# Rotary tiles rotated one by one through three places, evictions in another order, six mixing banks, and the softmax weights of both heads on VectorE

## The reference

```python
proj = rmsnorm_2(x, norm_g) @ w_in
(a_q, a_k, a_v, a_g, b_q, b_k, b_v, b_g, i_q, i_k, i_w, c_q, c_k, c_v, c_g, m_g) = split(proj)
ya = moba_attention(rope(a_q), rope(a_k), a_v) * silu(a_g)             # 6 heads: causal softmax here
yb = dsa_attention(rope(b_q), rope1(b_k), b_v, rope(i_q), rope1(i_k), i_w) * silu(b_g)   # 6 heads, 256 keys picked
# 12 heads in 3 groups of dilation 1, 4, 16; each gives an output o_g and a log-sum-exp lse_g:
yc = sum_g softmax_over_g(lse_g) * o_g                                 # "the mixing"
yc = yc * silu(c_g)
merged = sigmoid(m_g0)*(ya @ w_br_a) + sigmoid(m_g1)*(yb @ w_br_b) + sigmoid(m_g2)*(yc @ w_br_c)
x = x + merged @ w_out
# apply_rope: concat([x1*c - x2*s, x1*s + x2*c]) on the halves x1, x2 of each head's 64 channels
```

## Time and profile before

| | |
|---|---|
| median of 3 runs | 3239.16 us (3238.86 to 3243.96) |
| profiled execution, its own time | 3240.51 us |
| its span in the profile | 3238.8 us |
| TensorE (PE) busy | 3096.6 us (96%) |
| VectorE (DVE) busy | 1712.2 us (53%) |
| ScalarE (ACT) busy | 1190.6 us (37%) |
| GpSimd (POOL) busy | 251.5 us (8%) |
| mean granted TensorE clock | 0.98 |

### The profile page before, as it was taken

One profiled execution on the slowest core, in us unless ns is written; L12 is line 12 of the kernel. 1 busy time (PEld: TensorE's weight loads), 2 busy tenths in 40 slices (PEclk: granted clock), 3 DMA queues, 4 the chain that ended last, 5 costly groups with the idle time before them and its releaser, 6 DMA issues.

```text
span 3238.8 us, 38745 instructions
## 1 busy us (share of the span) xinstructions
PE 3096.6 (96%) x16353; PEld 2597.7 (80%) x16353; DVE 1712.2 (53%) x2370; ACT 1190.6 (37%) x1574; POOL 251.5 (8%) x324
## 2 busy tenths in 40 slices
PE   6999999999999999999999999899899999898999
PEld 5888888888888988888798888777777897676788
DVE  6555553345555653347753334688654357865434
ACT  3222255642122422236732223334562233455422
POOL 0000011210000000001200000122210001311000
PEclk8999999999999999999999999899999999999999
DMA  6555522114555352323222322332222224322222
GB/s 229 182 177 187 169 79 65 53 53 169 199 183 170 119 187 91 104 78 108 78 92 91 101 94 68 96 90 74 85 72 78 91 66 123 85 79 66 78 92 72
DMA packets 287270, 354.23 MB, mean 109 GB/s; under 512 B 9546, under 2 KB 263290, under 8 KB 287098
## 3 DMA queue, kind: packets, MB, share of 16 engines
q1 hardware_dynamic: 287098, 351.75, 33.6%
HBM read 336.52 MB, written 2.10 MB: 105 GB/s over the span
## 4 chain that ended last, share of the span: by engine, by line
PE 80%; DVE 11%; ACT 5%; POOL 1%; issue 1%; DMA 1%; SPq 0%; DVEq 0%; ACTq 0%; POOLq 0%
PE psum L655 50%; PE psum L814 6%; PE psum L1202 5%; PE psum L772 3%; PE psum L1294 3%; PE psum L676 2%; PE psum L696 1%; DVE w_low L1909 1%; ACT area L1709 1%; PE psum L912 1%; DVE area L2369 1%; PE psum L1176 1%; DVE area L2415 1%; DVE psum L2058 1%; DVE mod_acc L2425 1%
## 5 line engine op out<-in xcount | busy, mean ns | idle before, releaser
L655 PE MATMUL psum<-h_high,w_high 128*128 128x512 f32 (+1 forms) x1936 | 757.1, 391 | 8.0 <-DVE w_low L1909 5.0
L655 PE MATMUL psum<-h_high,w_low 128*128 128x512 f32 (+1 forms) x1936 | 753.4, 389 | 0.0
L655 PE MATMUL psum<-h_low,w_high 128*128 128x512 f32 (+1 forms) x1936 | 753.4, 389 | 0.0
L1909 DVE TENSOR_TENSOR w_low<-raw,w_high 128x2048 fp32r<-128x2048 f32 (+3 forms) x246 | 547.1, 2235 | 315.3 <-ACT w_high L1352 315.3
L1352 ACT CAST w_high<-raw 128x2048 fp32r<-128x2048 f32 (+4 forms) x254 | 464.8, 1843 | 570.2 <-DMA raw<-in_ffn_w_gu 237.4
L655 PEld LDWEIGHTS psum<-h_high,w_high 128*128 128x128 f32 (+1 forms) x1936 | 362.6, 187 | 88.9 <-issue 8.7
L655 PEld LDWEIGHTS psum<-h_high,w_low 128*128 128x128 f32 (+1 forms) x1936 | 362.6, 187 | 77.0
L655 PEld LDWEIGHTS psum<-h_low,w_high 128*128 128x128 f32 (+1 forms) x1936 | 362.7, 187 | 76.4 <-issue 1.0
L655 PE MATMUL psum<-y_high,w_high 128*128 128x512 f32 x592 | 233.0, 394 | 7.3 <-DVE y_low L2095 3.4
L2181 DVE TENSOR_TENSOR area<-area,psum 128x512 f32<-128x512 f32 x88 | 60.2, 684 | 336.9 <-PE psum L655 328.5
L655 PE MATMUL psum<-y_high,w_low 128*128 128x512 f32 x592 | 231.4, 391 | 0.0
(11 more groups left out here) (312 smaller groups left out, 5185.4 us busy)
## 6 DMA issues: line engine op xcount, KB each, us to landing
raw<-in_ffn_w_gu SPq DMA_DIRECT2D x88, 1024.0 KB, 6.1
raw<-in_mod_w SPq DMA_DIRECT2D x64, 1024.0 KB, 5.0
raw<-in_w_in SPq DMA_DIRECT2D x64, 1024.0 KB, 5.2
raw<-in_ffn_w_down SPq DMA_DIRECT2D x32, 1024.0 KB, 7.5
raw<-in_ffn_w_down SPq DMA_DIRECT2D x16, 768.0 KB, 4.8
raw<-in_sb_w_qkv SPq DMA_DIRECT2D x12, 1024.0 KB, 5.2
area<-area SPq DMA_DIRECT2D x92, 128.0 KB, 2.3
raw<-in_lru_w_in SPq DMA_DIRECT2D x10, 1024.0 KB, 5.4
```

The costliest lines, as they stand in the source:

```text
L655: mm = e.matmul(psum[0:width, base + m, :], wv[a][:, at_k, c0:c0 + width], X[b][:, k, :], start=(at_k == 0 and (a, b) == (0, 0)), stop=(at ...
L1909: e.tensor_tensor(w_low[raw_at[m]][:, :n], raw[raw_at[m]][:, :n], w_high[x % NW][:, :n].bitcast(F32), ALU.subtract).then_inc(*q.up(s_low, ...
```

## The change

1. **Three places by tiles.** The tiles to be rotated or turned in the heads go round through three places (`L.x_at`): the two of `rope_x` and one more. A tile waits only for the tile three before it (`x_tile_free`, `tile_left`). The swap is of one tile, four DMAs of half the size, with a semaphore for each half of `rope_y`; it waits for the eviction and for the previous rotated unit's same half (`y_tile_free`).
2. **VectorE's rotations** (`rope_tile`) of all that was made beside p-1 stand together in round p, behind `row_max` and ahead of `lows` and `weights`. GpSimd's `rope_begin` waits for the eviction and no longer for the swap.
3. **Evictions.** ScalarE evicts turned values at the head of the round where they lead the list; only one product, and only in rounds with more than two items beside, is evicted between the two `exps`; the other products of the first list are evicted behind `turned_copy(p)`.
4. **Weights.** VectorE scales both heads' weights; GpSimd's `weights` is gone.
5. **Mixing.** The three pairs of banks are taken at once and all six matmuls are issued in a row.

```diff
@@ -565,10 +572,37 @@
...
+            places = [L.rope_x[:, 0, :], L.rope_x[:, 1, :], spare(0, 5, 6)[:, 0, :]]
+            in_heads = [(name, c0, m) for name, c0 in order[order.index(("a_v", 256)) + 1:] for m in range(2)]
+            L.x_at = {tile: places[i % 3] for i, tile in enumerate(in_heads)}
+            def tile_left(name, c0, m):
+                if name == "c_v" or (name, c0, m) == ("b_q", 256, 1):
+                    turned = [("tile_turned", stage, name, c0, m)]
+                    if name == "c_v":
+                        return turned
+                else:
+                    turned = []
+                return turned + [("swapped", stage, name, c0, m), ("rope_cos", stage, name, c0, m)]
+            def x_tile_free(name, c0, m):
+                at_ = in_heads.index((name, c0, m))
+                if at_ >= 3:
+                    return tile_left(*in_heads[at_ - 3])
+                return x_left("a_v", 256) + x_left("a_k", 128)
+            def y_tile_free(name, c0, m):
+                before = rotated[rotated.index((name, c0)) - 1]
+                return [("roped", stage, *before, m)]
+            L.x_tile_free, L.y_tile_free = x_tile_free, y_tile_free
...
-                return [x_left(*order[-1]), y_left(*rotated[-1]), [("past", (stage, "heads"), x) for x in ENGINES]][b]
+                return [[step for tile in in_heads[-3:] for step in tile_left(*tile)], [("roped", stage, *rotated[-1], m) for m in range(2)], [("past", (stage, "heads"), x) for x in ENGINES]][b]
@@ -1260,16 +1292,17 @@
...
+                pairs = [take_pair() for _ in range(3)]
+                q.wait_ge(*at("mix_weights", stage))
+                q.wait_ge(*at("mix_sel", stage))
...
-                    b = base_of["mix", stage, m] = take_pair()
-                    q.wait_ge(*at("mix_weights", stage))
-                    q.wait_ge(*at("mix_sel", stage))
...
-                        if g == 2:
-                            q.wait_ge(*at("mixed", stage, m, 0))
-                        e.matmul(psum[:, b + g % 2, :], L.sel[0:4, m, :], L.lse_rows[g], start=True, stop=True).then_inc(
+                        bank = base_of["mix", stage, m, g] = pairs[m] + g if g < 2 else pairs[2] + m
+                        e.matmul(psum[:, bank, :], L.sel[0:4, m, :], L.lse_rows[g], start=True, stop=True).then_inc(
...
-                    free_pair(b, ("mixed", stage, m, 2))
+                    free_pair(pairs[m], ("mixed", stage, m, 2))
+                free_pair(pairs[2], ("mixed", stage, 1, 2))
@@ -1736,14 +1769,12 @@
...
-                        for before in L.x_free(name, c0):
+                        for before in L.x_tile_free(name, c0, m):
...
-                        dst, dil = L.rope_x[:, m, :], L.dilation(name, c0) if what == "rope" else (1, 4, 16)[c0 // PANEL]
+                        dst, dil = L.x_at[name, c0, m], L.dilation(name, c0) if what == "rope" else (1, 4, 16)[c0 // PANEL]
...
-                        if what == "rope" and last:
-                            q.mark("roped_in", stage, name, c0)
@@ -1789,25 +1820,36 @@
...
-                    first = L.beside[p][0]
+                    first, second = L.beside[p]
+                    turned = [item for item in first if item[0] == "turn"]
+                    made = [item for item in first if item[0] == "product"]
+                    needed = made[:1] if made[:1] == first[:1] and len(first) + len(second) > 2 else []
...
+                    if first[:1] == turned[:1]:
+                        for item in turned:
+                            evict(*item)
...
-                    for item in first[:1]:
+                    for item in needed:
...
-                    for item in first[1:]:
-                        evict(*item)
+                    if first[:1] != turned[:1]:
+                        for item in turned:
+                            evict(*item)
...
+                    for item in made:
+                        if item not in needed:
+                            evict(*item)
@@ -2392,6 +2434,25 @@
...
+                def rope_tile(name, c0, m):
+                    dil, rows = L.dilation(name, c0), L.parts(name, c0)[m]
+                    src, cos, sin = L.x_at[name, c0, m][0:rows, :], rope_c[0:rows, :], L.rope_y[0:rows, m, :]
+                    to = L.dests[name, c0][m][0:rows, :]
+                    if dil > 1:
+                        src, cos, sin = (a.rearrange("p (j r) -> p j r", r=dil) for a in (src, cos, sin))
+                        to = to.rearrange("p (r j) -> p j r", r=dil)
+                    if m:
+                        q.wait_ge(*at("evicted", stage, "product", name, c0, m))
+                        if (name, c0) in L.place_of:
+                            for x in range(2):
+                                q.wait_ge(*at("scores_taken", stage, L.place_of[name, c0], x))
+                        e.tensor_tensor(to, src, cos, ALU.mult).then_inc(*q.up(s_vec, "rope_cos", stage, name, c0, m))
+                    q.wait_ge(*at("swapped", stage, name, c0, m))
+                    e.tensor_tensor(L.rope_y[0:rows, m, :], L.rope_y[0:rows, m, :], rope_s[0:rows, :], ALU.mult).then_inc(*q.up(s_vec))
+                    q.wait_ge(*q.newest)
+                    q.wait_ge(*at("rope_cos", stage, name, c0, m))
+                    e.tensor_tensor(to, to, sin, ALU.add).then_inc(*q.up(s_vec, "roped", stage, name, c0, m))
@@ -2431,8 +2492,6 @@
...
-                    if x:
-                        return
@@ -2505,7 +2558,8 @@
...
-                    beside(L.done(p - 1, 1))
+                    for tile in L.to_rotate(p - 1, 0) + L.to_rotate(p - 1, 1) if p >= 0 else ():
+                        rope_tile(*tile)
@@ -2515,7 +2569,6 @@
...
-                    beside(L.done(p, 0))
@@ -2528,10 +2581,9 @@
...
-                    b = base_of.get(("mix", stage, m), 0)
...
-                        e.tensor_tensor(L.og[g][m], L.og[g][m], psum[:, b + g % 2, :], ALU.mult).then_inc(*q.up(s_vec, "mixed", stage, m, g))
+                        e.tensor_tensor(L.og[g][m], L.og[g][m], psum[:, base_of.get(("mix", stage, m, g), 0), :], ALU.mult).then_inc(*q.up(s_vec, "mixed", stage, m, g))
@@ -2754,25 +2806,23 @@
...
-                def beside(units):
-                    for name, c0 in units:
-                        if L.what(name, c0) == "rope":
-                            place = L.place_of.get((name, c0))
-                            rope_cos(name, c0, *([] if place is None else [("scores_taken", stage, place, x) for x in range(2)]))
-                def weights(p):
-                    buf, m0 = L.SS[2 * (p % 2) + 1], 16 * (2 * (p % 2) + 1)
-                    q.wait_ge(*at("one_over", stage, p, 1))
-                    for w, (a, b) in L.spans(p):
-                        m = e.tensor_scalar(buf[:, a:b], buf[:, a:b], L.stat[:, m0 + 12 + w:m0 + 13 + w], None, ALU.mult)
-                    m.then_inc(*q.up(s_pool, "weights", stage, p, 1))
+                def rope_begin(name, c0):
+                    q.wait_ge(*at("evicted", stage, "product", name, c0, 0))
+                    if (name, c0) in L.place_of:
+                        for x in range(2):
+                            q.wait_ge(*at("scores_taken", stage, L.place_of[name, c0], x))
...
-                    beside(L.done(p - 1, 1))
-                    if p + 1 < len(L.pairs):
-                        weights(p + 1)
-                    beside(L.done(p, 0))
+                    for name, c0, m in L.to_rotate(p - 1, 0) + L.to_rotate(p - 1, 1) if p >= 0 else ():
+                        if m == 0:
+                            rope_begin(name, c0)
@@ -2912,9 +2962,15 @@
...
-                    for name, c0 in L.done(p, w):
-                        if L.what(name, c0) == "rope":
-                            swap(name, c0)
+                    for name, c0, m in L.to_rotate(p, w):
+                        q.wait_ge(*at("evicted", stage, "product", name, c0, m))
+                        for step in L.y_tile_free(name, c0, m):
+                            q.wait_ge(*at(*step))
+                        for r in range(0, L.parts(name, c0)[m], HD):
+                            for a, b in ((r, r + 32), (r + 32, r)):
+                                e.dma_start(L.rope_y[a:a + 32, m, :], L.x_at[name, c0, m][b:b + 32, :]).then_inc(
+                                    *q.up(s_swap_tile[m], "swapped", stage, name, c0, m, by=16))
```

More of the change, by code:

```diff
@@ L125, in build @@
         s_end = sem("end_gain_loaded")
+        s_swap_tile = [sem(f"swapped_tile{i}") for i in range(2)]
         s_first = [sem(f"first_mods{i}") for i in range(KD)]
@@ L488, in done, with to_rotate @@
                 return [(name, c0) for how, name, c0, m in L.beside[p][w] if how == "product" and m == last_tile(name, c0)]
-            L.begun, L.done, L.last_tile = begun, done, last_tile
+            def to_rotate(p, w):
+                if p < -1:
+                    return []
```

(2 more changed lines are left out.)

15 lines of the change are left out of this document (7 added, 8 removed).

## The result

The changed kernel takes 3187.05 us (median of 4 runs, 3186.33 to 3190.32) against 3239.33 (4 runs): a ratio of 0.9839, 95% interval 0.9827 to 0.9851. That is 52.3 us less; the forecast was 57.2 less, and the time lies inside its range. The profiled execution took 3190.32 us, the slowest of the four.

What follows compares the result with a forecast made beforehand. TensorE was taken as the bound, with VectorE taking over in rounds 0 to 3. Terms 22.0 + 2.8 + 4 = 28.8 us a layer, 57.6 for two, gave 3182 us; range 3166 to 3209.

Steps and rivals of the forecast that it cites:

- Rounds 4 to 9: Heads: TensorE's waits for copies and turned `c_v` 512 go, 17.0 us plus 5 of clock, 22.0 us a layer.
- VectorE as the bound of rounds 0 to 3: Heads: `take_scores(4)` only 5.0 us earlier, new wait of 8.3 at the turn of `c_v` 256; net 2.8 us a layer.
- Part 4: VectorE scaling head 1's weights: loss of 3.6 us in three rounds, already in the sum; upper end 10 a layer.
- Part 5: Mixing: six products in a row win 4 us a layer, between 0.8 and 6.7 by where the clock falls.
- The swaps: Rounds 0 to 3: a one-tile swap takes as long as a two-tile swap, 4.2 us, giving VectorE stalls of 3.7.
- the other reading: Swap DMAs: if cost went with size, stalls would fall to some 1.5 us and the total to 3178.
- A: Rival, 15%: VectorE doesn't hold TensorE in round 3; 13.3 instead of 2.8 us won a layer, 3161 us, half 3171.
- B: Rival, 22%: VectorE or SP late in the heads' second half too; 10 us lost a layer, 3202, up to 3210.
- C: Rival, 5%: late swaps of four tiles a layer reach TensorE and make the kernel slower; 3250 us at 8.5 lateness.
- L: How much later than 4.2 us each of four swaps a layer lands; from 7.2 us on the kernel is slower.
- D: Rival, 4%: the waits only change place and nothing reaches the end, 3239 us.
- Signs: Expected in the profile: `take_scores` without idle in rounds 1 to 3, rotations waiting 1 to 3 us, six gapless mixing products.

Runs made afterwards that it cites:

- order_alone: The kernel before with ScalarE's new order of evictions alone; places by whole units, rotations and mixing as before: 3189.7 us, ratio 0.9847.
- sel_late: The changed kernel with VectorE's gate selection steps later, 5, 2, 2, 6, 8 in rounds 0 to 4: 3169.3 us, ratio 0.9784.
- pool_weights: The changed kernel with head 1's weights scaled on GpSimd again, as before the change: 3176.8 us, ratio 0.9807.
- tile_behind: The changed kernel with the third of three tiles rotated together moved behind the round's `w_low` on VectorE: 3179.4 us, ratio 0.9815.
- order_mix: The kernel before with only ScalarE's new order of evictions and the six mixing banks: 3177.1 us, ratio 0.9808.
- mix_alone: The kernel before with only the six mixing banks and the six products in a row: 3224.1 us, ratio 0.9953.

## Why the prediction was right, and where it was not

- **Forecast and range.** 57.2 us less were forecast, 52.3 came. In the profile the heads won 24.3 and 23.0 us a layer where the sum had 22.0 + 2.8 = 24.8, and products and first branch 2.9 and 3.9 where it had 4. The two terms of the heads can be told apart where TensorE starts the scores of pair 5, at the head of round 4 (h0, before and then after):

```profile
2263.70 1.16 PE L1112 MATMUL psum<-area,y_plain 64*128 64x128 f32 x16
...
2264.35 1.16 PE L1146 MATMUL psum<-area,y_plain 64*128 64x128 f32 x16
```

  From the heads' start that is 115.8 us before and 113.5 now: 2.2 us won up to there (1.6 in h1) where the sum had 2.8, and 22.1 from there on (21.4 in h1) where it had 22.0.
- **Rounds 4 to 9.** Right in size: the waits behind 3.9, 1.7, 7.4 and 4.0 us of the sum are gone but for 0.3. Wrong was what the 22.0 were laid to, parts 1 and 3 together: order_alone shows that the copies' going first does it without the finer places, for the waits for places that are left behind them are of 0.2 us in those rounds.
- **VectorE as the bound of rounds 0 to 3.** Right in place and size: a wait of 8.3 at the turn of `c_v` 256 was forecast, 8.9 and 9.5 came, and sel_late, pool_weights and tile_behind each shrink it by relieving VectorE alone. `take_scores(4)` came 99.4 - 95.8 = 3.6 us earlier against the heads' start, not 5.0. Behind `take_scores(1)` VectorE lost 2.2 us to GpSimd's products, which the sum did not have, and 4.3 instead of 3.7 to stalls, and stood idle for `scores(2)` for 0.5 instead of 1.9; these three make up the 1.4. What stands from there to the scores of pair 5, the clock with it, cost 1.4 us more than before where 2.2 were counted, which hides part of that. That the eviction hangs on the exponentials was half of it: the cast ahead of them is held as well.
- **Part 4** was sized 3.6 us a layer and cost 5.2, with some 3 to either side. The term was made from durations taken while GpSimd was still; the rows show what that leaves out.
- **Part 5** was sized 4 a layer. It came to 2.9 and 3.9 in the changed kernel's profile, and to 6.3 (order_mix against order_alone, some 3 to either side) and 7.6 (mix_alone, 5.7 to 9.7) by the medians. So 4 was too low for the part alone, by mix_alone. It was the middle between two cases of before, and where among the six products the clock falls, which decides between them, the prediction could not tell; nor can the runs.
- **The swaps.** The cost of a 64 KB swap was kept near that of 128 KB, and the stalls came out at 4.3 us rather than the 1.5 of the other reading. The DMA issues of the changed kernel (count, KB each, median us to landing) stand beside the 2.3 us for 128 KB. The Trainium skill ("DMA: Bandwidth & Descriptors", Rules for kernel authors) says of transfers under 64 KB that one pays mostly overhead; these are at that size and twice it, and the trace agrees in so far as half the bytes took 0.3 us less:

```profile
area<-area SPq DMA_DIRECT2D x88, 64.0 KB, 2.0
```

- **Rivals.** A fell (the wait came). B fell: no wait for VectorE in rounds 4 to 9 of either layer. C fell: the longest stall's swap took 4.6 us from its first issue to use (2198.77 to 2203.37 in h0) where 4.2 was taken, so L was 0.4, and tile_behind, in whose h0 no rotation waits for a swap, puts what the stalls cost at 7.7 us in all. D fell by the time.
- **Signs.** `take_scores(1)` to `(4)` stood idle once, for 0.50 us; the rotations waited four times for a swap in h0, 0.8 to 2.7 us; six products without a gap; no scaling on GpSimd.

Stage by stage the sum held within 2 us a layer, the terms 22.0 and 2.8 and the wait of 8.3 among them, so the total is not luck. Its stages show 3.5 of the 4.9 us by which the forecast was too fast; the rest is within the scatter of the profiles. Inside rounds 0 to 3 two errors of about 1 us offset each other, as said. Priced by edits rather than by stage, part 5 is worth more than its term and part 4 may cost more than its own; these prices depend on what else is in the kernel and don't add up to the 52 us.

## What to carry to other kernels

When a copy that the bottleneck waits for stands behind one that waits for a buffer, put it first before you cut the buffer finer: the order alone won 50 us where the whole change won 52, and the finer places, with the rotations that go with them, nothing that could be measured until another engine's work was moved. Once a wait is gone, look for the engine whose arrival ends the next one and give it less in those rounds; here eight small steps moved to a later round were worth 18 us, and moving 1.2 us a round onto that engine cost 10. A part that wins nothing today may be what a later edit needs, so try parts again when the bound has moved.

## What the runs showed of the hardware

- VectorE slows beside GpSimd when both work in SBUF: the rotation's product that started at 2176.31, 0.13 us behind a GpSimd product of 1.37, took 1.79 us instead of 0.68. Its end, 2178.10, is 0.55 behind the end of GpSimd's, 2177.55. The Trainium skill ("SBUF — State Buffer", SBUF: two separate sides) says that a VectorE operation with two SBUF inputs and a GpSimd one that reads SBUF exclude each other for the whole instruction; these two rows agree with it, and so do the two `w_low` of 5.59 us, longer by 1.1, beside the GpSimd product at 2206.06, which itself took 2.50 us instead of 1.29. The scalings have one SBUF input, so that sentence does not cover them; their 2.08 us are longer by 0.8.
- The granted clock fell from 2.4 to 1.2 GHz while TensorE was busy without a gap: in the changed kernel's h0 behind four mixing products of 4 rows (0.95, then 0.50 in the two stretches above; 1.00 in the 6 us of 128x512 products ahead of them), in mix_alone's only behind the sixth (0.97, then 0.50). What decides where it falls was not found; between these two it is worth 2 us in the mixing products.
- The start of the heads scattered by up to 9 us between profiles of kernels that do not differ ahead of it.
